# Forgetting attention: turned probabilities made by products with a diagonal of the inverse sums

## The reference

```python
proj = h @ w_qkvf                      # q, k, v (1024 each) and 16 forget logits
log_f = log_sigmoid(f_logit + b_f)
cum = cumsum(log_f over the tokens)    # per head
# for each block of 128 queries, keys 0 .. q1:
logits = einsum("bqhd,bkhd->bhqk", qb, kb) * HEAD_DIM ** -0.5
logits = logits + cum[:, :, q0:q1, None] - cum[:, :, None, :q1]
logits = where(causal mask, logits, neg)
p = softmax(logits, axis=-1)
outs.append(einsum("bhqk,bkhd->bqhd", p, vb))
...
o @ w_o
```

## Time and profile before

| | us |
|---|---|
| median of 3 runs | 3607.75 (3607.05 to 3609.73) |
| the profiled execution | 3612.2 |
| its span, first to last instruction | 3610.5 |
| TensorE busy | 3544.7 (98%) |
| VectorE busy | 2041.8 (57%) |
| ScalarE busy | 1534.3 (42%) |
| GpSimd busy | 323.8 (9%) |
| GpSimd's scaling in the attention (L2678), 64 instructions | 68.4 |
| granted TensorE clock, mean | 0.992 |

### The profile page before, as it was taken

How to read it: one execution, slowest core, us unless ns; L and a number is a source line. 1 busy time by engine, 2 the same in 40 slices (tenths; PEclk the granted TensorE clock), 3 DMA queues, 4 the chain that set the end, 5 groups by cost and what they waited for, 6 DMA issues and landing times. The chain is left out here.

```text
span 3610.5 us, 49501 instructions
## 1 busy us (share of the span) xinstructions
PE 3544.7 (98%) x20379; PEld 2922.8 (81%) x20379; DVE 2041.8 (57%) x2881; ACT 1534.3 (42%) x2459; POOL 323.8 (9%) x307
## 2 busy tenths in 40 slices
PE   8999999999999999999999999999999999999998
PEld 6888788888788888887778778888988887877887
DVE  5987687775534454446686663444364744355743
ACT  5674678543423332222553432233453323275322
POOL 3772000000000000002111000000000000043000
PEclk9999999999999999999999999999999999999999
DMA  6345644333333333333320233333223333411332
GB/s 203 100 135 172 200 130 142 113 95 94 88 94 99 94 94 99 97 94 96 96 74 3 77 100 98 95 95 104 88 82 97 96 95 93 141 48 53 94 98 83
DMA packets 597624, 365.34 MB, mean 101 GB/s; under 512 B 16887, under 2 KB 578887, under 8 KB 596887
## 3 DMA queue, kind: packets, MB, share of 16 engines
q1 hardware_dynamic: 592807, 350.43, 32.7%
q10 hardware_dynamic: 4592, 11.73, 0.8%
HBM read 345.70 MB, written 15.89 MB: 100 GB/s over the span
## 5 line engine op out<-in xcount | busy, mean ns | idle before, releaser
L1363 PE MATMUL later_bank<-arena 128*128 128x512 f32 (+1 forms) x6792 | 1435.2, 372 | 9.8 <-DVE arena L1311 6.5
L1363 PEld LDWEIGHTS later_bank<-arena 128*128 128x128 f32 x6792 | 1193.1, 188 | 245.7 <-DVE arena L1311 14.2
L1303 ACT ACTIVATE arena<-arena 128x1024 fp32r<-128x1024 f32 (+3 forms) x545 | 566.2, 1039 | 1529.2 <-PE later_bank L1363 751.4
L1363 PE MATMUL middle_bank<-arena 128*128 128x512 f32 x4896 | 1125.7, 391 | 2.6 <-DVE arena L1311 1.1
L1363 PEld LDWEIGHTS middle_bank<-arena 128*128 128x128 f32 x4896 | 915.7, 187 | 211.3 <-issue 13.5
L1311 DVE TENSOR_TENSOR arena<-arena 128x1024 fp32r<-128x1024 f32 (+2 forms) x547 | 662.3, 1211 | 543.0 <-ACT arena L1303 536.5
L1363 PE MATMUL front_bank<-arena 128*128 128x512 f32 (+3 forms) x1776 | 350.0, 356 | 3.4 <-DVE arena L1311 2.6
L1363 PEld LDWEIGHTS front_bank<-arena 128*128 128x128 f32 (+1 forms) x1776 | 291.2, 188 | 59.4 <-DVE arena L1311 5.3
L1556 POOL TENSOR_TENSOR arena<-arena 128x512 f32<-128x512 f32 x120 | 171.2, 1426 | 113.8 <-ACT arena L1868 97.6
L1363 PE MATMUL ssd_bank<-arena 128*128 128x512 f32 x576 | 145.1, 403 | 0.0
L2025 DVE SCALAR_TENSOR_TENSOR arena<-front_bank,columns,arena 128x510 f32<-128x510 f32 (+1 forms) x224 | 126.8, 628 | 18.3 <-ACT arena L1795 16.7
(11 more groups left out here) (486 smaller groups left out, 3022.2 us busy)
## 6 DMA issues: line engine op xcount, KB each, us to landing
arena<-in_w_in SPq DMA_DIRECT2D x114, 512.0 KB, 3.8
arena<-in_ffn_w_gate SPq DMA_DIRECT2D x76, 512.0 KB, 3.7
arena<-in_ffn_w_up SPq DMA_DIRECT2D x76, 512.0 KB, 3.7
arena<-in_w_mlp SPq DMA_DIRECT2D x64, 512.0 KB, 3.8
arena<-in_w_ada SPq DMA_DIRECT2D x48, 512.0 KB, 5.8
arena<-in_ffn_w_down SPq DMA_DIRECT2D x48, 512.0 KB, 4.0
arena<-scratch_cum SPq DMA_DIRECT2D x64, 256.0 KB, 6.3
arena<-in_gm_w_in SPq DMA_DIRECT2D x32, 512.0 KB, 3.8
```

Source lines behind the costliest of these rows:

```text
L1303: act.activation(self.high[q % self.AHEAD][:, 0:kb * cols], self.raw[self.slot(g)][:, 0:kb * cols], ACT.Copy).then_inc(self.high_done, 1)
L1363: ins = pe.matmul(out, still, moving, start=first and n_pass == 0, stop=last and n_pass == 2)
```

## The change

GpSimd no longer scales the rows of exponentials. It scales the 128x128 identity with the same column instead, into one of four new 128x128 tiles (`inverses`), and first waits until the turn of four steps before has used that tile. TensorE no longer transposes: it multiplies the unscaled rows (stationary) by this diagonal, which turns and scales a tile in one float32 product. The turned tiles of pairs A and B (`BY_VECTOR`) are copied by VectorE at its step m + 6 (`TAKE_AFTER`), behind the maximum and the inverse and ahead of o_low in the program of a step; those of C and D stay with ScalarE. The semaphore of the copies is split in two, and TensorE waits for the one that counts.

```diff
-    NJ, BUFS, TURN_AFTER = 2 * CH, 8, 4
+    NJ, BUFS, TURN_AFTER, TAKE_AFTER = 2 * CH, 8, 4, 6
+    BY_VECTOR = (0, 1)
...
+        self.inverses = [arena.f(NORMED_AT + self.BUFS + 4, 1)[:, 0, n * P:(n + 1) * P] for n in range(4)]
...
+    def wait_copied(self, pe, j, half):
+
+        by_vector = j % CH in self.BY_VECTOR
+        same = [n for n in range(j) if (n % CH in self.BY_VECTOR) == by_vector]
+        pe.wait_ge(self.copied_dve if by_vector else self.copied_act, 2 * len(same) + half + 1)
...
# pool
         for m in range(DB * NJ):
-            n = (self.step(m)[2] + 1) * P
-            buf = self.s[m % self.BUFS][:, 0:n]
             pool.wait_ge(self.inverted, m + 1)
-            pool.tensor_scalar(buf, buf, self.rden[:, m % NJ:m % NJ + 1], None, ALU.mult).then_inc(self.normed, 1)
+            if m >= 4:
+                pool.wait_ge(self.p_turned, m - 3)
+            pool.tensor_scalar(self.inverses[m % 4], self.rg.core.ident[:], self.rden[:, m % NJ:m % NJ + 1], None, ALU.mult).then_inc(self.normed, 1)
...
# tensor, turn(j)
                 if j:
-                    pe.wait_ge(self.p_copied, m - 1)
+                    self.wait_copied(pe, j - 1, half)
                 for n in range(j % CH + 1):
-                    ins_ = pe.transpose(pt_banks[half][:, n * P:(n + 1) * P], self.s[m % self.BUFS][:, n * P:(n + 1) * P], core.ident[:])
+                    ins_ = pe.matmul(pt_banks[half][:, n * P:(n + 1) * P], self.s[m % self.BUFS][:, n * P:(n + 1) * P], self.inverses[m % 4],
+                                     start=True, stop=True)
...
# tensor, weighted_sums(j)
-            pe.wait_ge(self.p_copied, 2 * j + 2)
+            self.wait_copied(pe, j, 1)
...
# scalar
-            if 0 <= done < last:
+            if 0 <= done < last and step(done)[2] not in self.BY_VECTOR:
...
-                act.activation(self.p_t[done % 4][:, 0:n], pt_banks[done % 2][:, 0:n], ACT.Copy).then_inc(self.p_copied, 1)
+                act.activation(self.p_t[done % 4][:, 0:n], pt_banks[done % 2][:, 0:n], ACT.Copy).then_inc(self.copied_act, 1)
...
# vector, behind the inverse of step m - 1
+            done = m - self.TAKE_AFTER
+            if 0 <= done < last and step(done)[2] in self.BY_VECTOR:
+                n = (step(done)[2] + 1) * P
+                dve.wait_ge(self.p_turned, done + 1)
+                if done >= 4:
+                    dve.wait_ge(self.pv_done, done // 2 - 1)
+                dve.tensor_copy(self.p_t[done % 4][:, 0:n], pt_banks[done % 2][:, 0:n]).then_inc(self.copied_dve, 1)
             b, left = divmod(m - self.TURN_AFTER - 2 - NJ, NJ)
```

More of the change, by code:

```diff
@@ L2630, in __init__ @@
         self.inverted, self.normed = sem("sums_inverted"), sem("probs_normed")
-        self.p_turned, self.p_copied, self.pv_done = sem("probs_turned_done"), sem("probs_copied"), sem("pv_products")
+        self.p_turned, self.pv_done = sem("probs_turned_done"), sem("pv_products")
+        self.copied_act, self.copied_dve = sem("probs_copied_by_scalar"), sem("probs_copied_by_vector")
         self.high_done, self.low_done = sem("o_high"), sem("o_low")
@@ L2826, in vector @@
         resid, s = core.resid, self.s
-        score_banks, o_banks = (rg.banks[0], rg.banks[1], rg.banks[4], rg.banks[5]), rg.banks[6:8]
+        score_banks, pt_banks, o_banks = (rg.banks[0], rg.banks[1], rg.banks[4], rg.banks[5]), rg.banks[2:4], rg.banks[6:8]
         order = Order(dve, self.order)
```

## The result

The changed kernel takes 3635.56 us (median of 4 runs, 3628.60 to 3638.28) against 3607.86 us before: ratio 1.0073, 95% interval 1.0061 to 1.0085. It is slower by 28 us. Measured again beside other kernels it gave 1.0079 (1.0065 to 1.0093). The forecast was 3629 us in a range of 3618 to 3636; for the profiled execution it was 3633.9, and that took 3636.2. The median lies only 0.4 us inside the upper end of the range.

What follows compares the result with a forecast made beforehand. Bound: TensorE's 8.75 us a block plus 0.65 idle from the ring o_high, o_low, score maximum. Six blocks +17.3, filling +2.1, emptying +2.3 make +21.7 us: profiled execution 3633.9, median 3629 us, range 3618 to 3636.

Steps and rivals of the forecast that it cites:

- Products at L2736's pace: Attention loop, TensorE: 160 products replace transposes, each 0.228 us like the filler products; work per block 8.75 to 10.93 us.
- T_D: TensorE's turn of row pair D (four tiles, two halves): eight products take 1.98 us instead of 1.02.
- T_C: TensorE's turn of row pair C (three tiles, two halves): 1.52 us with products, 1.03 before.
- T_A: TensorE's turn of row pair A (one tile, two halves): 0.61 us with products, 0.37 before.
- Rivals 2 and 4: Attention loop: 2, GpSimd is the hidden limit, 3603 us, chance 0.05; 4, a product costs four transposes, 3659 us, 0.02.
- A's second copy behind o_low: VectorE's queue: the copy waits behind o_low and D's second maximum; TensorE idles 1.35 us a block.
- T_B: TensorE's turn of row pair B (two tiles, two halves): 1.07 us with products; its second half, 0.61, waits for A's copy.
- Rival 1: Attention loop: the new wait doesn't bite, TensorE's work sets 10.93 to 11.1 us a block; 3620 us, chance 0.17.
- the path: Chain through one block, TensorE's groups, then o_high, o_low, D's maximum and A's copy: 12.35 us instead of 9.47.
- Filling and emptying: Loop's start up to the first o_high, +2.1 us; its end after the seventh o_high, +2.3 us.
- rival 3: TensorE's clock falls in each block's 1.35 us idle stretch: +5 to +10 us on top, 3637 us, chance 0.13.
- its new wait: GpSimd waits for the turn four steps back before reusing a diagonal; over 4 us past when it comes, cost zero.

Runs made afterwards that it cites:

- the second run: The changed kernel, unaltered, measured again beside other kernels on the same chip: 3634.49 us, ratio 1.0079 to the kernel before.

## Why the prediction was right

Forecast +2.88 a block, measured +3.08. The mechanism held: the products' pace, and the copy behind o_low. That the time fell inside the range, and the profiled execution so near its forecast (3636.2 and 3633.9), is partly luck: its loop grew by 4.4 us more than forecast and began 2.0 us earlier than before, and one more fall of the clock would have put the median outside. The steps:

- **Products at L2736's pace.** T_D 1.98 forecast and measured, T_C 1.52 and 1.53, T_A 0.61 and 0.64. The row of the same form in the same loop was the right one to take; a record's length (273 and 275 ns) would have said that nothing changes. Rivals 2 and 4 fall with this.
- **A's second copy behind o_low.** From o_high to T_B's second half 2.28 us forecast, 2.34 measured; TensorE idles 1.32 us there (1.35 forecast), ended by VectorE's copy. The kernel with the copies one step earlier shows that the place makes it. Rival 1 falls: its block of 10.93 to 11.1 is what the order kept the changed kernel from, and 11.08 came when the copies and o_low were both moved.
- **What the path left out.** It named one way to the copy. The second, over the reciprocal and the exponential, is shorter (12.06 us a block when it decides) and did not show until o_low was moved. The forecast held since the longer one was named.
- **Small terms.** T_B's second half is 0.68 and not 0.61, T_A 0.64; with the handovers 0.2 a block, 1.2 us in all.
- **Filling and emptying.** From the first scores to the first o_high 19.5 before and 21.9 after: +2.35, forecast +2.1. From the seventh o_high to the end 8.7 and 10.8: +2.1, forecast +2.3, with the fall of the clock that was expected.
- **The clock.** This was rival 3, on top of the forecast and not in place of it: two falls in six blocks at 1.6 us each, 3.2 us, fewer than the half to all of the blocks that it named; one in the second run. Its sign, a clock of 0.50 between 3220 and 3290, came. It is the largest part of what the forecast missed in the loop (+21.7 forecast, +26.1 measured), and the sum had no term for it between no fall and half of the blocks.
- **GpSimd.** That its new wait costs nothing held, but not for the reason given. It isn't over 4 us past: GpSimd waits for the turn 32 times, 38.2 us in all. No idle time of a TensorE record is put down to it; TensorE's weight loads wait, in time that the stall or the products cover.
- **The base.** I put the median 4.5 us under the profiled execution, as before. After the change the two were alike (3635.56 and 3636.23). That distance makes most of the gap between 3629 and 3635.6. I take it for chance of one execution, since those of the kernel before on one other chip spread from 3604.0 to 3614.2.

By the Trainium skill's page TensorE: Matmul & The Clock Gate, section Terms, transposes in float32 are 4 times faster; here they are twice as fast (0.108 and 0.228), in the loop as in the fillers. Its section Part 4: PE-mode transpose says that transposes don't count as activity for the clock. The runs don't decide it: over 3202 to 3282 us the clock stood at 1.00 before the change, but there the transposes take only about a third of TensorE's time. That products would give the end's 1.7 us back they don't bear out: the clock fell at the loop's end in one trace of six with transposes and in two of seven with products.

## What to carry to other kernels

When an instruction is moved to an engine with free time, write down everything ahead of it in that engine's queue and what each of those waits for; the free share says nothing about its place. Here one step of place was worth 12.8 us of loop, some 4.6 of them falls of the clock. The move itself lost 1.3 even at the better step (98.4 against 97.1 with all copies on ScalarE); 96.2 came only with o_low moved as well, and ScalarE's copies with o_low moved weren't tried. Cost a replaced operation by a row of the same form under the same conditions, back to back, and not by the length of one record. And where an engine is 91% busy, ask for the chain before relieving it: the 0.5 us a block that could be had lay in o_low's place, found by following the idle time of TensorE.

## What the runs showed of the hardware

A float32 product of 128x128 by 128x128 takes 0.228 us back to back and a transpose of the same tile 0.108, though single records of both last 273 to 275 ns. A stall of 1.32 us in a loop that is otherwise full was followed by 3.4 us at 1.2 GHz in two blocks of six, one of six in a second run and none of six with fillers in it, which one execution doesn't show to be the fillers' doing. Two kernels with the same waits of 0.81 and 0.95 us in their last T_C had a fall behind them in one trace and none in the other; one such fall cost 1.6 us here, more than the stall.
